# A hybrid attention block in float32: the output projection with activations as the stationary operand, its result by token in eight PSUM banks

## The reference

```python
u = rmsnorm(h, norm_mix_g)
rq, rk, rv, rg, cq, ckv, kr = split(u @ w_in)
ret_out = silu(rg) * head_groupnorm(retention(rq, rk, rv), ret_out_g)      # 8 heads of 128
mla_out = rmsnorm(latent_attention(cq, ckv, kr), mla_out_g)               # 8 heads of 128
h = h + concat([ret_out, mla_out]) @ w_o                                  # 2048 x 2048
m = rmsnorm(h, norm_mlp_g)
h = h + square(relu(m @ w_up)) @ w_down                                   # 2048 x 8192 x 2048
return rmsnorm(h[frames], final_norm_g)
```

## Time and profile before

| | |
|---|---|
| median of 3 runs | 1121.18 us |
| profiled execution | 1123.17 us |
| its span, first to last instruction | 1121.4 us |
| TensorE busy | 98% |
| VectorE, ScalarE, POOL busy | 79%, 60%, 6% |
| granted clock, mean | 0.997 of full |
| DMA, mean over the span | 184 GB/s |

### The profile page before, as it was taken

The page is one execution under the profiler, slowest core; times in us unless marked ns, Lnnn a source line. Parts: engine busy times, 40 slices in busy tenths (PEclk is TensorE's granted clock), DMA queues, the critical chain, the costliest instruction groups (busy, mean ns, idle before and its releaser), DMA issues.

```text
span 1121.4 us, 15786 instructions
## 1 busy us (share of the span) xinstructions
PE 1098.9 (98%) x6136; PEld 953.1 (85%) x6136; DVE 882.8 (79%) x1222; ACT 673.8 (60%) x1012; POOL 66.4 (6%) x78
## 2 busy tenths in 40 slices
PE   7999999999989999999999999999999999999997
PEld 6899999999878888888788888788888778888885
DVE  6986877777687667689887979887879986888965
ACT  7665666666656555556665555656556656556644
POOL 0001110111204330000000000000000000000000
PEclk9999999999999999999999999999999999999999
DMA  9544444444345545555565555565554655555651
GB/s 363 213 151 150 156 146 151 151 150 150 128 172 193 184 150 188 189 188 188 193 225 183 188 188 184 197 220 188 188 188 171 232 196 188 188 188 188 242 208 75
DMA packets 29592, 206.89 MB, mean 184 GB/s; under 512 B 3408, under 2 KB 3664, under 8 KB 5200
## 3 DMA queue, kind: packets, MB, share of 16 engines
q1 hardware_dynamic: 29232, 205.59, 53.1%
q10 hardware_dynamic: 288, 0.31, 0.1%
HBM read 203.79 MB, written 2.10 MB: 184 GB/s over the span
## 4 chain that ended last, share of the span: by engine, by line
PE 86%; DVE 7%; ACT 4%; issue 1%; DMA 1%; SPq 0%; POOL 0%; POOLq 0%; DVEq 0%
PE acc L392 62%; PE ps_kn L392 5%; PE ps_x L392 4%; PE ps_v L392 4%; PE ps_qn L392 4%; PE ps_qr L392 4%; PE ps_y L392 3%; DVE lo L1178 3%; DVE t_raw L1178 2%; ACT hi L813 1%; ACT t_hi L813 1%; DVE t_lo L1178 1%; ACT kept L813 1%; DMA x_in<-x_all 1%; DVE raw L1178 1%
## 5 line engine op out<-in xcount | busy, mean ns | idle before, releaser
L392 PE MATMUL acc<-xs,hi 128*128 128x512 f32 (+1 forms) x1952 | 587.5, 363 | 0.0
L1178 DVE TENSOR_TENSOR lo<-raw,hi 128x1024 fp32r<-128x1024 f32 (+1 forms) x379 | 460.8, 1219 | 116.7 <-ACT hi L813 112.8
L813 ACT ACTIVATE hi<-raw 128x1024 fp32r<-128x1024 f32 (+1 forms) x379 | 396.5, 1050 | 181.5 <-PE acc L392 90.0
L392 PE MATMUL acc<-xs,lo 128*128 128x256 f32 (+1 forms) x1648 | 455.2, 285 | 8.2 <-DVE xs L1212 6.9
L392 PEld LDWEIGHTS acc<-xs,hi 128*128 128x128 f32 x1952 | 346.0, 190 | 52.2
L392 PEld LDWEIGHTS acc<-xs,lo 128*128 128x128 f32 x1648 | 312.1, 189 | 15.3 <-issue 6.8
L813 ACT ACTIVATE half_b<-acc 128x256 f32<-128x256 f32 x100 | 38.4, 384 | 138.3 <-PE acc L392 138.3
L392 PE MATMUL acc<-hid,hi 128*128 128x512 f32 x256 | 91.8, 399 | 0.0
L392 PE MATMUL ps_kn<-hi,act_p 128*128 128x512 f32 x192 | 75.2, 392 | 1.3 <-ACT kept L813 1.3
L392 PE MATMUL acc<-hid,lo 128*128 128x256 f32 x256 | 69.4, 281 | 0.0
L1178 DVE TENSOR_TENSOR t_lo<-t_raw,t_hi 128x1536 fp32r<-128x1536 f32 x28 | 49.2, 1759 | 11.8 <-ACT t_hi L813 11.8
(11 more groups left out here) (316 smaller groups left out, 1406.3 us busy)
## 6 DMA issues: line engine op xcount, KB each, us to landing
raw<-w_up SPq DMA_DIRECT2D x64, 1024.0 KB, 4.9
raw<-w_down SPq DMA_DIRECT2D x64, 1024.0 KB, 4.9
raw<-w_in SPq DMA_DIRECT2D x42, 1024.0 KB, 4.9
raw<-w_o SPq DMA_DIRECT2D x16, 1024.0 KB, 5.0
h_res<-x_frames SPq DMA_DIRECT2D x1, 2048.0 KB, 8.1
x_in<-x_all SPq DMA_DIRECT2D x3, 544.0 KB, 8.1
consts<-consts_in SPq DMA_DIRECT2D x1, 1218.5 KB, 9.3
raw<-w_in SPq DMA_DIRECT2D x2, 512.0 KB, 9.5
```

What stands on the lines that cost most here:

```text
L392: return pe.matmul(o, l, m, start=start, stop=stop)
L813: return act.activation(o, i, ACT.Copy)
L1178: return dve.tensor_tensor(o, a, b, op)
```

## The change

The output projection holds the activations stationary. Chunks 0 to 7 of `w_o` are now one tile of `hid` each (128 of the 2048 inputs) with all 2048 output features: 4 groups of 512 features, 2 token groups of 128, which fills all eight PSUM banks (`wo_acc`). Chunks 8 to 15 hold four tiles for one group of 512 features each, two chunks a group, so that a group is finished every two chunks. VectorE adds a finished group to the residual, which is loaded straight into `res` as token by feature (`h_add`). One chunk later TensorE transposes it back into the group's own two banks (`wo_turn`, 8 transposes), from where ScalarE (`m_round`) and VectorE (`m_rest`) write the MLP's input. ScalarE squares the rows of `res` with a running sum per token (`h_square`); VectorE puts the sums on the diagonal of two tiles (`diag`, in place of `sq`), and a matmul of `ones` with them spreads the sum over the partitions. POOL has no part in the stage. The first up block is cut in two, steps 0 to 5 and 6 to 15, with the last group's transposes in between. Around the entry, `split_lo` of chunk `C_WO`, the MLA scaling and rounding and the retention norm of head 7 stand at other places.

```diff
-            def wide(c, b, wide_of, hi_of, ..., span=(0, KT), ready=None, late=False):
+            def wide(c, b, wide_of, hi_of, ..., span=(0, KT), ready=None):
...
-                narrow(("v", h), ready=inside({10: mla_total}) if early else None)
+                narrow(("v", h), ready=inside({12: mla_total}) if early else None)
...
-            for span in ((0, HEADS - 1), (HEADS - 1, KT - 1), (KT - 1, KT)):
-                for j in range(2):
-                    wo_block(j, span=span, ready=lambda k, j=j: mixed(k, j), late=j == 1)
...
-            turn(0)
-            for j in range(2, KT):
-                wo_block(j)
-                turn(j - 1)
+            def wo_turn(g):
+
+                pe.wait_ge(sem["ht"], TILES * (g + 1))
+                for j in range(PER_CHUNK):
+                    for t in range(TILES):
+                        m = pe.transpose(wo_acc[g][j // 2][:, j % 2 * FRAMES + t * P:j % 2 * FRAMES + t * P + P],
+                                         res[:, t, g * GROUP + j * P:g * GROUP + j * P + P], ident)
+                    m.then_inc(sem["ht_ps"], 1)
...
+            for k in range(WO_ALL):
+                c = C_WO + k
+                wo_ready(k)
+                for g in range(GROUPS):
+                    if g % 2 == 0:
+                        pe.wait_ge(sem["lo_ready"], 2 * c + g // 2 + 1)
+                    for t in range(TILES):
+                        if k == 0 and g == 1 and t == 0:
+                            ret_var(HEADS - 1)
+                            pe.wait_ge(sem["acc_read"], BLOCK_OF[LAST])
...
+                        m = product(wo_acc[g][t], wo_act(k, t), unit(c, g), k == 0, False)
+                    if g % 2 == 1:
+                        m.then_inc(sem["chunk_used"], 1)
+            for g in range(GROUPS):
+                for n in range(WO_PARTS):
+                    c = C_WO + WO_ALL + WO_PARTS * g + n
+                    k0 = WO_ALL + PER_CHUNK * n
+                    pe.wait_ge(sem["lo_ready"], 2 * c + 2)
+                    for t in range(TILES):
+                        for j in range(PER_CHUNK):
+                            wo_ready(k0 + j)
+                            m = product(wo_acc[g][t], wo_act(k0 + j, t), unit(c, j), False,
+                                        n == WO_PARTS - 1 and j == PER_CHUNK - 1)
+                            if t == TILES - 1 and j == 1:
+                                m.then_inc(sem["chunk_used"], 1)
+                        if n == WO_PARTS - 1 and t == 0:
+                            m.then_inc(sem["wo_ps"], 1)
+                    m.then_inc(sem["chunk_used"], 1)
+                    if n == 0 and g:
+                        wo_turn(g - 1)
...
-                    wide(c0 + j, b0 + j, x_wide, x_hi, ready=m_parts if s == 0 and j == 0 else None)
                     if s == 0 and j == 0:
-                        turn(KT - 1)
-                        pe.wait_ge(sem["h_ss"], KT)
-                        mm(ps_x[:, 0:FRAMES], ones, sum_sq[:]).then_inc(sem["h_ss_ps"], 1)
+                        pe.wait_ge(sem["m_lo"], KT - PER_CHUNK)
+                        wide(c0, b0, x_wide, x_hi, last=False, span=(0, 6))
+                        wo_turn(GROUPS - 1)
+                        wide(c0, b0, x_wide, x_hi, first=False, span=(6, KT), ready=m_parts)
+                        pe.wait_ge(sem["h_ss"], TILES)
+                        mm(ps_qn[:, 0:FRAMES], ones, diag[:]).then_inc(sem["h_ss_ps"], 1)
+                    else:
+                        wide(c0 + j, b0 + j, x_wide, x_hi)
```

SyncE, between the fourth and the fifth chunk of `w_o`:

```diff
-            sp.wait_ge(sem["mla_o_ps"], HEADS)
-            sp.wait_ge(sem["ret_o_ps"], HEADS)
-            sp.dma_start(h_res[:], x_frames).then_inc(sem["x_back"], 16)
+                    for done in ("mla_o_ps", "ret_o_ps", "gate_exp", "gate"):
+                        sp.wait_ge(sem[done], HEADS)
+                    sp.dma_start(res[:], x_frames).then_inc(sem["x_back"], 16)
```

ScalarE, in the stage and in the first up block:

```diff
+            for k in range(KT):
+                split_hi(C_WO + k + 2, 0)
+                split_hi(C_WO + k + 2, 1)
+                if k == 1:
+                    ret_round(g)
+                if 1 <= k <= 4:
+                    for n in range(2):
+                        mla_round(2 * k - 2 + n)
+                n, part = divmod(k - WO_ALL, WO_PARTS)
+                if n >= 1 and part == 0:
+                    h_square(n - 1)
+                if n >= 1 and part == 1:
+                    m_round(n - 1)
+            m_round(GROUPS - 1)
+            h_square(GROUPS - 1)
...
+                    if s == 0 and j == 0:
+                        act.wait_ge(sem["h_sq"], TILES * GROUPS)
                     b_copy(c0 + j, w0 + j)
```

VectorE, at the entry, in the stage and in the first up block:

```diff
             c = CHUNK_OF["v", g]
-            split_lo(c + 2, 0)
             ret_norm(g - 1)
             dve.wait_ge(sem["mla_sd"], 1)
             dve.reciprocal(rstd[:], rstd[:]).then_inc(sem["mla_rstd"], 1)
             dve.wait_ge(sem["chunk_used"], 2 * c + 2)
             tt(rv[:], acc[BLOCK_OF["v", g] % 2][:, 0:TOK], rstdx[:], ALU.mult).then_inc(sem["acc_read"], 1)
-            dve.wait_ge(sem["mla_rstd"], 1)
-            for k in range(3):
-                mla_scale(k)
+            ret_rest(g - 1)
+            split_lo(c + 2, 0)
             ret_in(g)
...
+            def h_add(g):
+                for t in range(TILES):
+                    if t == 0:
+                        dve.wait_ge(sem["wo_ps"], g + 1)
+                    else:
+                        dve.wait_ge(sem["chunk_used"], 2 * (C_WO + WO_ALL + WO_PARTS * (g + 1)))
+                    part = res[:, t, g * GROUP:(g + 1) * GROUP]
+                    tt(part, wo_acc[g][t][:], part, ALU.add).then_inc(sem["ht"], 1)
+
+            def m_rest(g):
+                for j in range(PER_CHUNK):
+                    n = PER_CHUNK * g + j
+                    dve.wait_ge(sem["m_hi"], n + 2 - j % 2)
+                    dve.scalar_tensor_tensor(out=xs[:, n, TOK + META:], scalar=gain(G_MLP + n),
+                                             in0=wo_acc[g][j // 2][:, j % 2 * FRAMES:(j % 2 + 1) * FRAMES],
+                                             in1=xs[:, n, META:TOK].bitcast(F32), op0=ALU.mult,
+                                             op1=ALU.subtract).then_inc(sem["m_lo"], 1)
+
+            for k in range(KT):
+                split_lo(C_WO + k + 2, 0)
+                if k == 0:
+                    for n in range(HEADS):
+                        mla_scale(n)
+                if k == 1:
+                    ret_norm(g)
+                split_lo(C_WO + k + 2, 1)
...
+                n, part = divmod(k - WO_ALL, WO_PARTS)
+                if n >= 1 and part == 1:
+                    m_rest(n - 1)
+                if n >= 0 and part == 1:
...
+                    h_add(n)
+            m_rest(GROUPS - 1)
...
                     sum_ab(z[:], b0 + j, w0 + j).then_inc(sem["acc_read"], 1)
                     if s == 0 and j == 0:
+                        dve.wait_ge(sem["h_sq"], TILES * GROUPS)
+                        dve.tensor_reduce(fin_pre[:], fin_ss[:], AX.X, ALU.add).then_inc(sem["h_sum"], 1)
+                        dve.wait_ge(sem["h_sum"], 1)
+                        for t in range(TILES):
+                            dve.tensor_scalar(diag[:, t * P:t * P + P], ident, fin_pre[:, t:t + 1], None,
+                                              ALU.mult).then_inc(sem["h_ss"], 1)
                         dve.wait_ge(sem["h_sd"], 1)
```

More of the change, by code:

```diff
@@ L40 @@
 C_GATE7 = CHUNK_OF[LAST]
[L41 to L42 removed]
+C_WO = len(PLAN)
+C_MLP, B_MLP, W_MLP = C_WO + KT, len(BLOCK_OF), len(HALF_OF)
 SEGS = 4
@@ L392, in mm, with wide @@
                 return pe.matmul(o, l, m, start=start, stop=stop)
-            def wide(c, b, wide_of, hi_of, more=0, bmore=0, first=True, last=True, span=(0, KT), ready=None, late=False):
+            def wide(c, b, wide_of, hi_of, more=0, bmore=0, first=True, last=True, span=(0, KT), ready=None):
                 a = acc[b % 2]
@@ L412, in wide @@
                         m = mm(a[:, FRAMES:], wl, hi_of(k), False, False)
-                    if n % 8 == 7 and not (late and n == 7):
-                        m.then_inc(sem["chunk_used"], 2 if late else 1)
+                    if n % 8 == 7:
+                        m.then_inc(sem["chunk_used"], 1)
             def x_wide(k):
@@ L655, in _, with product, unit, wo_ready @@
                 3: lambda: ret_scores(HEADS - 1), 13: lambda: ret_values(HEADS - 1)}))
[L658 to L667, removed]
+            def product(o, x, w, first, last):
+                mm(o[:], x[0], w[0], first, False)
+                mm(o[:], x[0], w[1], False, False)
+                return mm(o[:], x[1], w[0], False, last)
+            def unit(c, j):
+                return hi[c % 2][:, j * GROUP:(j + 1) * GROUP], lo[c % 2][:, j * GROUP:(j + 1) * GROUP]
+            def wo_ready(k):
                 tile = WO_ORDER[k]
-                if tile == 3 and j == 1:
-                    ret_var(HEADS - 1)
                 if tile < HEADS:
```

(15 more changed lines are left out.)

118 lines of the change are left out of this document (50 added, 68 removed).

## The result

The changed kernel took **1126.24 us** (median of 8 runs, 1124.91 to 1126.96), the kernel before 1122.67 us in 8 runs on the same chip (1120.78 to 1123.31). The ratio is 1.0038, 95% interval 1.0029 to 1.0048: 0.4% slower, a small difference but clear of the noise. The profiled execution took 1126.91 us, its span 1125.0; against the profiled execution of before that is +3.74, and +3.6 in span.

The account below looks back on a forecast made before the run. The prediction took TensorE, busy 98% of the span, as the bound. Its terms, -4.1 - 1.6 - 1.9 + 0.3 + 4.4 + 2.6 + 1.6 + 1.6 = +2.9 on 1123.17, gave 1126.0 us, range 1123.0 to 1128.0.

Parts of the forecast that it names:

- entry: Last V block into the output stage: waits before head 7's scores and for MLA squares go, with the clock dip; -4.1 us.
- first transposes: Start of the output stage: TensorE no longer turns a block straight after it is summed, so its wait goes; -1.6 us.
- matmuls: Output projection: 24 matmuls of 512 columns a chunk take 5.48 us where the old block took 5.60; -1.9 us.
- waits inside: Within the output stage: sq_lo of head 7 and h_add for groups 1 and 2 each about 0.1 late; +0.3 us.
- first gap: Before the first up block: TensorE waits for group 2's low parts, m_rest(2) behind a weight split on VectorE; +4.4 us.
- second gap: After the first up block: TensorE waits for the two diagonal tiles, behind VectorE's split, z and reduction; +2.6 us.
- clock: Behind both exit gaps: TensorE's granted clock dips once after each; +1.6 and +1.6 us, the first from 1.0 to 2.5.
- rival of the column rule: Output projection: 24 matmuls of 512 run no faster than 16 pairs of 512 and 256; 1127.9 us, chance 0.05.
- rival with none: Stage exit: the clock stays up over both gaps, so the kernel is not slower; 1122.7 us, chance 0.08.
- rival with one fall: Stage exit: the second gap leaves the clock up, so only one dip; 1124.4 us, chance 0.27.
- Slow low parts: Output stage and exit: m_rest takes its old 0.875 us for a reason other than POOL; 1130.8 us at worst, chance 0.07.

Follow-up runs that it names:

- e5: Kernel before with only VectorE's split of chunk c+2, part 0, moved behind rv: 1118.82 us, ratio 0.9971.
- (B): Group of 24 matmuls in probe e8 on the changed kernel: head-tile slices starting 16 elements further on stationary, weights moving; 0.2329 us each.
- e1: Changed kernel with m_round(n-1), m_rest(n-1) and h_add(n) put between the two weight-split parts, ahead of the second: 1124.59 us, ratio 1.0019.
- e6: Changed kernel with m_round(n-1), m_rest(n-1) and h_add(n) put ahead of both weight-split parts: 1120.34 us, ratio 0.9982.
- e2: Changed kernel with h_square(3) ahead of m_round(3), and the reduction and diagonal right behind m_rest(3): 1123.07 us, ratio 1.0005.
- e4: Changed kernel with unused matmuls filling TensorE's exit waits, 17 ahead of the first and 8 ahead of the second: 1123.15 us, ratio 1.0008.
- e9: Changed kernel plus a second probe of 96 matmuls with other operands before the first up block: groups at 0.2329, 0.2333, 0.2271 and 0.2338 us a matmul.
- e8: Changed kernel plus a first probe of 96 matmuls in four operand groups before the first up block: 0.2308, 0.2329, 0.2346 and 0.2279 us a matmul.
- e10: Changed kernel plus a third probe of 96 matmuls with other operand starts before the first up block: 0.2279, 0.2267, 0.2296 and 0.2288 us a matmul.

## Why the prediction was right

Step by step, in the profiled executions, on the clock of the span. The stage lasts from 318.09 to 410.13, 92.04 us; before, from 322.86 to 417.68, 94.82.

| step | forecast | measured |
|---|---|---|
| entry | -4.1 | -4.03 (19.32 to 15.29) |
| first transposes | -1.6 | -1.8 with its signal |
| matmuls | -1.9 | **-0.6** |
| waits inside | +0.3 | +0.1 (sq_lo; the turns show none) |
| first gap | +4.4 | +4.13 |
| second gap | +2.6 | +2.32 |
| clock | +1.6 and +1.6 | **+2.53** and +1.60 |
| turns, longer first matmul behind each | 0 | +0.1 |
| sum | +2.9 | +4.4 |

From this 0.72 us is to be taken, by which everything was earlier in this execution long before the change (the first matmul with x_sq starts at 33.14, and at 33.86 before): that gives the 3.7 seen.

**The entry** was right in mechanism and size, and e5 isolates it. **The waits inside** were not seen at the transposes; where a turn was to be 0.1 late, nothing shows.

**The matmuls** are the term that was mis-sized. The step took 0.2285 us from the down stage for "this form". The nine chunks from 324.08 to 374.03, between which no turn stands, recur every 5.55 us, 0.2313 a matmul; over the whole stage a chunk comes to 5.56 against the old 5.60, not to 5.48. The probes give 0.2267 to 0.2346 for matmuls of this size with little changed but their operands, so a pace read off one stage does not hold for another with other operands. That it is the start of the head-tile slices which costs the 0.08 per chunk is likely but not shown, as (B) has it. By the formula of the Trainium skill (TensorE: Matmul & The Clock Gate, "Back-to-back issue gap") for the gap of a single matmul, 512 columns would take 0.216 us, and the section gives 0.131 for a sustained stream with weight loads; no group here came under 0.2267, so the measurement decides. The rival of the column rule forecast no gain at all; the 0.6 measured lies nearer to it than to the 1.9 of the sum.

**The first gap** had the right length, for a reason that was half told. The prediction named the second half of the split of C_WO + 17. Its chain is there: ScalarE has the second half from 410.32, VectorE's part of it is followed by m_rest at 412.55, and the sum from the chunk's end is right. But the first half stood in front too. Its turn on VectorE came only at 410.09: TensorE frees that half of the buffer when six of the last chunk's eight products are done, and ScalarE's part (409.00, 1.06 us) comes first. e1 took the second half away and left 2.66 of 3.98; e6 took both away, on ScalarE as well as on VectorE, and left nothing. My expectation for e1 failed on exactly this.

**The second gap** is as described (e2). **The clock**: e4 shows that TensorE's having no matmul is the cause. The first fall cost 2.53 us, at the upper bound given, since the six slow steps are followed by eight transposes in 1.38 us for 0.79; the second 1.60. In the profiled execution of the changed kernel both falls occurred, and both again in e1, so the rival with none is out. The rival with one fall is out for that execution and not for all: e9 and three runs of e6 show a second gap that cost no clock. The sum counted it in full, and that this fits the profiled execution is in part luck.

**Slow low parts** did not occur: m_rest came every 0.39 us. The section of the Trainium skill that the prediction cites for it (SBUF — State Buffer, "SBUF: two separate sides") has a second condition beside two SBUF inputs, a two-port mode. POOL had no work in the stage, so no run here tests either.

The total, 1126.0 for 1126.24, is better than its parts: the matmuls 1.3 too optimistic, the clock 0.9 too low, against 0.6 too much on the gaps, 0.7 of chance in the start-up, and a median that lies 0.7 under the profiled execution of the changed kernel.

## What to carry to other kernels

Where one engine's order interleaves work for the next stage with work that an engine is waiting for, look at what its queue does in its idle time before the deadline: here VectorE idled 3.89 us and ScalarE 2.63 with a group ready in its banks, and moving some small operations and the diagonal ahead of splits nobody wanted yet turned +3.6 us into -6.1 (1116.21 against 1122.35 beside it) with the same arithmetic. Look at both engines of such a pair: m_rest cannot begin before m_round, which had its turn on ScalarE only at 411.28, and e6 moved both. Take a gap of TensorE at its length plus the slow steps behind it (4.13 + 2.53 here, and 2.4 + 1.7 for the second, whose slow steps do not come in every execution). And time a change in pieces: the one moved line of e5 gives 3.5 of those 6.1 us by itself, the new stage 2.6, and the slower whole had hidden both.

## What was unexpected of the hardware

The pace of matmuls of 512 columns, each with a stationary slice of 128, depends, among other things, on where their operands begin. One head-tile slice used 24 times took 0.2329 us a matmul when it began 64 bytes into its buffer (E), and 0.2279 when it began at 6656 bytes, a multiple of 256 (I); a weight slice 64 bytes off took 0.2333 (F), one 256 bytes off 0.2267 (J). The rule behind it is open, since B, half of whose slices begin at multiples of 256 bytes, took 0.2329. Moving the head tiles to other places was not tried.

The clock fell behind gaps of 4.13, 2.81 (e1), 2.44 (e6) and 2.32 us. It fell behind a gap of 2.44 us in e8 and e10 and not in e9, so that at this length the executions of one order differ. It did not fall behind e5's wait of 1.61 us for the first residual block, nor when 17 matmuls of no use filled the first gap.
